# Weight slots of a two-block fp32 kernel, spread over four places within 256 bytes

## The reference

```python
z = rms_norm(h) @ w_in                         # 2048 x 11264
merged = gate_a * (y_a @ w_branch_a) + gate_b * (y_b @ w_branch_b)
h = h + merged @ w_out                         # 2048 x 2048
h = h + square(relu(rms_norm(h) @ w_up)) @ w_down   # 2048 x 8192 x 2048
proj = rmsnorm(concat([meta, rms_norm(h)])) @ w_in_2   # 272 tokens, 2048 x 6656
y = concat([ya, yb]) @ w_out_2                 # 2048 x 2048
```

## Time and profile before

| what | value |
|---|---|
| median of 2 runs | 1893.53 us (1892.76 to 1894.31) |
| the profiled execution, its own time | 1891.33 us |
| its span, first to last instruction | 1889.5 us |
| PE busy | 1874.0 us, 99% |
| PEld (weight loads) busy | 1739.9 us, 92% |
| DVE busy | 1101.6 us, 58% |
| ACT busy | 889.1 us, 47% |
| POOL busy | 149.8 us, 8% |
| DMA packets, mean | 184 GB/s |
| mean granted TensorE clock | 0.999 of full speed |

### The profile page before, as it was taken

The page is one execution under the profiler, slowest core; times in us unless marked ns, Lnnn a source line. Parts: engine busy times, 40 slices in busy tenths (PEclk is TensorE's granted clock), DMA queues, the critical chain, the costliest instruction groups (busy, mean ns, idle before and its releaser), DMA issues.

```text
span 1889.5 us, 33863 instructions
## 1 busy us (share of the span) xinstructions
PE 1874.0 (99%) x13420; PEld 1739.9 (92%) x13420; DVE 1101.6 (58%) x1270; ACT 889.1 (47%) x1171; POOL 149.8 (8%) x133
## 2 busy tenths in 40 slices
PE   9999999999999999999999999999999999999998
PEld 9989998999999889988998899899889999899986
DVE  6655766567655555555445544554565556767664
ACT  6534444455544445443444344344454345674543
POOL 1001322411001100000010000001010000000000
PEclk9999999999999999999999999999999999999999
DMA  8656555566565656656665665566556665354454
GB/s 274 192 179 172 183 179 177 166 198 182 166 232 191 215 183 179 196 197 192 196 192 193 193 193 192 193 194 190 189 180 179 178 180 155 111 164 146 156 191 143
DMA packets 176915, 347.75 MB, mean 184 GB/s; under 512 B 11152, under 2 KB 11360, under 8 KB 176256
## 3 DMA queue, kind: packets, MB, share of 16 engines
q1 hardware_dynamic: 174176, 337.76, 57.2%
q0 software_dynamic: 2608, 8.08, 1.7%
HBM read 342.37 MB, written 2.10 MB: 182 GB/s over the span
## 4 chain that ended last, share of the span: by engine, by line
PE 96%; DVE 2%; ACT 1%; issue 0%; DMA 0%; SPq 0%; DVEq 0%; ACTq 0%
PE ps L445 58%; PE ps L457 33%; PE ps L547 1%; DVE wlo L1288 1%; PE ps L770 1%; PE ps L737 1%; PE ps L760 1%; ACT whi L886 0%; PE ps L780 0%; DMA raw<-in_w_in_dram 0%; PE ps L475 0%; PE ps L748 0%; PE ps L598 0%; PE ps L590 0%; DVE xlo L1310 0%
## 5 line engine op out<-in xcount | busy, mean ns | idle before, releaser
L1288 DVE TENSOR_TENSOR wlo<-raw,whi 128x1024 fp32r<-128x1024 f32 x631 | 796.7, 1269 | 694.2 <-ACT whi L886 693.2
L886 ACT ACTIVATE whi<-raw 128x1024 fp32r<-128x1024 f32 x631 | 664.3, 1058 | 882.7 <-PE ps L445 552.5
L445 PE MATMUL ps<-xhi,whi 128*128 128x256 f32 (+1 forms) x1904 | 541.5, 284 | 0.2 <-DVE wlo L1288 0.2
L445 PE MATMUL ps<-xhi,wlo 128*128 128x256 f32 (+1 forms) x1904 | 530.9, 279 | 0.0
L445 PE MATMUL ps<-xlo,whi 128*128 128x256 f32 x1664 | 462.1, 278 | 0.0
L445 PEld LDWEIGHTS ps<-xhi,whi 128*128 128x128 f32 x1904 | 359.2, 189 | 8.4 <-issue 6.5
L445 PEld LDWEIGHTS ps<-xhi,wlo 128*128 128x128 f32 x1904 | 357.8, 188 | 0.0
L445 PEld LDWEIGHTS ps<-xlo,whi 128*128 128x128 f32 x1664 | 313.0, 188 | 1.3 <-issue 0.5
L445 PE MATMUL ps<-x2hi,whi 128*128 128x256 f32 x1024 | 282.8, 276 | 0.0
L445 PE MATMUL ps<-x2lo,whi 128*128 128x256 f32 x1024 | 282.7, 276 | 0.0
L445 PE MATMUL ps<-x2hi,wlo 128*128 128x256 f32 x1024 | 282.7, 276 | 0.0
(11 more groups left out here) (371 smaller groups left out, 2368.5 us busy)
## 6 DMA issues: line engine op xcount, KB each, us to landing
raw<-in_w_in_dram SPq DMA_DIRECT2D x279, 512.0 KB, 3.8
raw<-in_w_up_dram SPq DMA_DIRECT2D x128, 512.0 KB, 3.7
raw<-in_w_down_dram SPq DMA_DIRECT2D x128, 512.0 KB, 3.6
raw<-in_w_out_dram SPq DMA_DIRECT2D x64, 512.0 KB, 4.0
raw<-in_w_branch_a_dram SPq DMA_DIRECT2D x16, 512.0 KB, 4.7
raw<-in_w_branch_b_dram SPq DMA_DIRECT2D x16, 512.0 KB, 4.0
x_nat<-in_x_dram SPq DMA_DIRECT2D x4, 512.0 KB, 7.0
rel<-in_rel_turned_dram POOLq DMA_DIRECT2D x8, 256.0 KB, 4.3
```

The source lines that it names most:

```text
L445: ins = mm(outs[b], w[:, k % SLOTS, j, cols], v, start=start, stop=last and j == CK - 1 and i == 2, skip_group_check=True)
L886: f(whi[:, k % SLOTS], raw[:, k % SLOTS], ACT.Copy).then_inc(whi_ready, 1)
L1288: tt(wlo[:, k % SLOTS], raw[:, k % SLOTS], whi[:, k % SLOTS], ALU.subtract).then_inc(wlo_ready, 1)
```

## The change

Slots of `whi` and `wlo` are now 4,160 bytes apart and not 4,096, so that slot s starts 64·s bytes further on modulo 256. `raw` keeps its slots. Each of the two tensors is declared flat with the widened length, and the view with four slots is built by hand over it; `wlo` leaves out the last 64 bytes. The filler `x_place` is gone. From the declared sizes everything behind `whi` moves by 256 bytes, so slot 0 and the activation tiles keep their relation modulo 256: seen from the weight slot, an activation tile stands 192 bytes on for slot 0, 128 for slot 1, 64 for slot 2 and 0 for slot 3. The instructions of every engine, their order and their waits are as before; only addresses differ.

```diff
-X_PLACE = 48
+SLOT_STEP = 16
 ARENA_PLACE = 16
...
         raw = sb("raw", [P, SLOTS, CK, CW])
-        whi = sb("whi", [P, SLOTS, CK, CW], F32R)
-        wlo = sb("wlo", [P, SLOTS, CK, CW], F32R)
-        sb("x_place", [P, X_PLACE])
+        w_wide = [sb(name, [P, SLOTS * (CK * CW + SLOT_STEP) - pad], F32R) for name, pad in (("whi", 0), ("wlo", SLOT_STEP))]
+        whi, wlo = [bass.AP(v[:].tensor, v[:].offset, [list(v[:].ap[0]), [CK * CW + SLOT_STEP, SLOTS], [CW, CK], [1, CW]])
+                    for v in w_wide]
         xhi = sb("xhi", [P, KT, TM], F32R)
         xlo = sb("xlo", [P, KT, TM], F32R)
         sb("arena_place", [P, ARENA_PLACE])
```

## The result

The changed kernel takes 1930.85 us (1930.77 to 1930.92, 2 runs) against 1893.53: ratio 1.0199, 95% interval 1.0183 to 1.0216. It is 37.3 us slower. The forecast was no change, and 1930.85 lies above the range's 1925.

What follows compares the result with a forecast made beforehand. The prediction took the pitch of TensorE's matmuls to bound the kernel. Its terms, 0 for the splits, 0 for the DMAs and 0 for TensorE, left 1893.5 us, range 1878 to 1925.

Steps and rivals of the forecast that it cites:

- What bounds the kernel: Whole kernel: it ends when TensorE's matmuls have been issued; their pitch counts, 113.3 or 117.9 ns for 256 columns.
- The estimate of 1600 high matmuls: Input projections: some 1600 of 3 x 1664 matmuls of 256 columns stand on the higher level.
- The splits and the DMAs at zero: ScalarE's copy, VectorE's subtraction and the DMA writes to `raw`: the new places cost 0 us.
- TensorE at zero: TensorE's stationary read against its own moving read: new relations cost 0 us, bounded by 39.7 us loss and 87.8 gain.
- the 39.7 of its bound: TensorE's upper bound of loss, all three new relations high: 24.4 us for 256 columns, 3.2 for 272, 12.1 for 512.
- The second rival: TensorE: all three new relations high, 512-column matmuls 6 ns slower; slower by over 2%, 1933 us; chance 0.07.
- its sign: Sign of the big loss: three of four 24-matmul chunks take 2830 ns, not 2720; moving-weight chunks pass 2747 by 70.
- The mild cases: TensorE: one new relation goes high, 1907 us, chance 0.26; or rotation breaks the high level, 1888 us, chance 0.19.

Runs made afterwards that it cites:

- the uniform runs: Kernel before, all slots kept alike, activation tiles moved to 0, 64 or 128 bytes from the slots modulo 256: 1936.39, 1933.38 and 1946.23 us.
- the low part alone at 192: Changed kernel's 64-byte stagger given to the high part's slots only, low part's slots left uniform at 192: 1930.35 us, ratio 1.0199.

## Why the prediction was wrong, by its own steps

**What bounds the kernel** was right. TensorE's pitch sets the end, the two levels 113.3 and 117.9 ns exist, and PE still waits for nobody. The estimate of 1600 high matmuls was near: by the starts it is 64 chunks, 1536.

**The splits and the DMAs at zero** were right. The copy and the subtraction last as before in all slots, though `raw` and `whi` now differ in place, and all of the loss is found in the pitch.

**TensorE at zero** is the step that failed: the term measured 37.3 us, near the 39.7 of its bound. Its reasons have to be parted. That writes beside the reads do not disturb them stands: the changed kernel has other places for them, and slot 0 keeps 113 and 114 ns from matmul to matmul inside its chunks in the branches. "A start shifted by 64 bytes changes when they meet more than how often" was an argument without a row, and the uniform runs refute it: 113.3, 120.0, 117.8 and 118.6 or 120.0 ns for relations 192, 0, 64 and 128, with nothing else changed. "The level is not set by the addresses alone" was true, and the wrong thing followed from it: the low level at 192 is a state, and the places decide whether that state exists. One relation out of four that the trace never left was no evidence that the other three are like it. The exactness, which I took for a fixed cost, was that of a uniform layout. The Trainium skill, SBUF — State Buffer, section Who interferes with whom, has TensorE never wait on anyone, which would have made the term zero. The runs at the four relations, 113.3 to 120.0 ns, do not agree with that as far as TensorE's own two operands go. The Trainium skill, TensorE: Matmul & The Clock Gate, section Back-to-back issue gap, gives columns / 2.4 + 2.5 ns, for one matmul by itself. It leaves 4.1 ns of the 113.3 over, and these runs show that what lies above it moves with the places, by up to 6.7 ns more.

**The sizes.** The second rival, all three new relations bad, is what happened, and its sign came for 256 columns: three chunks of four take some 2830 to 2890 ns. With 512 columns two of four pass 2747 ns, by 48 and not 70. Its sum of 39.7 us came near by luck, by two errors against each other. For 256 columns it had 24.4 us, 8.1 a slot, and 31.1 were measured: slot 3 costs 7 ns a matmul and not 4.5 and took 12.3 us, so the level of 117.9 was no upper bound, slot 1 took 9.3, and slot 0, counted as unchanged, 1.6, since it stood high in some stages, among them the first MLP quarter. For 512 columns it had 12.1, at 6 ns for three slots, and 6.0 were measured: relations 128 and 64 cost 4.0 ns, slot 0 lost 1.4, and relation 0 is 0.6 ns better than 192 was before. For 272 columns it had 3.2, measured 2.0. It was given 0.07. Its "against", that it needs all three to be bad, took them for three independent chances; the row that should have weighed was that 113.3 is the lowest of all levels seen.

**The mild cases** did not come, and the rotation unlocks nothing for good: only relations 192 and 64 were seen low, and slot 0 between bad ones stands in either state, as it does in the kernel before.

## What to carry to other kernels

Where TensorE is the bound and a stationary and a moving fp32 operand stream together, treat their distance modulo 256 bytes as a parameter like a tile size: this one kernel was 2 to 3% slower at each of the other distances tried for all or most of its chunks. Which distance is best in another kernel is not shown. Keep one relation for all slots and tiles (the row steps here were whole multiples of 256 bytes; other steps were not tried), and read the result from pitches by slot and by stage, because a mean hides that four values and two states are mixed. Where a trace holds only one value of what a change varies, its silence bounds nothing; vary it once before giving it zero.

## What the runs showed of the hardware

- The pitch of 256-column fp32r matmuls with a weight load each depends on the places of TensorE's two operands: 113.3 or 117.8 ns at 192 and at 64 bytes, 118.6 or 120.0 at 128, 120.0 at 0. With 512 columns moving and 128 stationary it is 228.9 or 233.3 at 192, 233.3 at 64, 226.7 at 0. It repeats every 256 bytes (slots of the high part 256 bytes further apart: 1892.43 against 1893.62 us), and 16 bytes off 192 it is 118.9 or 117.8.
- At 192 the two levels are states. A single transpose of 0.11 us moves a stretch of up to 52 chunks from one to the other, and with two transposes the change reached through three later MLP quarters, 11 us for 0.2 us of work. What picks the state stays open: neither the count of small matmuls nor their parity does it, and at one place it differed between profiled executions of kernels that are the same up to there.
- Which mechanism makes the places collide was not measured. That two reads meet in the memory is an idea. Writes by ScalarE and VectorE are not it (120.0 ns at relation 0 with and without them), and that the low part alone at 192 gains nothing says that whatever it is spans several instructions.
